# Feed-forward pairs of a two-block kernel: four special steps of eight, banks drained by ScalarE and added by transfers

## The reference, cut to what matters

```python
D_FF = 4 * D_MODEL
        u = _rmsnorm(h, norm_mlp_g[layer])
        a = jnp.einsum('bsd,df->bsf', u, w_up[layer])
        a = jnp.square(jax.nn.relu(a))
        h = h + jnp.einsum('bsf,fd->bsd', a, w_down[layer])
    return _rmsnorm(h, norm_final_g)
```

## Time and profile before

| | |
|---|---|
| median of 3 runs | 2109.48 us (2109.46 to 2109.78) |
| the profiled execution's own time | 2109.17 us |
| its span in the profile | 2107.1 us |
| TensorE (PE) busy | 2087.0 us, 99% |
| VectorE (DVE) busy | 1442.8 us, 68% |
| ScalarE (ACT) busy | 1082.2 us, 51% |
| GpSimd (POOL) busy | 40.1 us, 2% |
| moved by DMA | 402.60 MB, 191 GB/s |
| granted TensorE clock | 0.999 of full speed |

### The profile page before, as it was taken

How to read it: one execution, slowest core, us unless ns; L and a number is a source line. 1 busy time by engine, 2 the same in 40 slices (tenths; PEclk the granted TensorE clock), 3 DMA queues, 4 the chain that set the end, 5 groups by cost and what they waited for, 6 DMA issues and landing times.

```text
span 2107.1 us, 24963 instructions
## 1 busy us (share of the span) xinstructions
PE 2087.0 (99%) x10059; PEld 1753.2 (83%) x10059; DVE 1442.8 (68%) x1872; ACT 1082.2 (51%) x1409; POOL 40.1 (2%) x50
## 2 busy tenths in 40 slices
PE   8999999999999999999999999999999999999998
PEld 6888888888888888888888888888888888888886
DVE  5878788875555776556554455566896796797684
ACT  5545555555444675554455454354544554454453
POOL 0000000000000020000000000000000000000000
PEclk9999999999999999999999999999999999999999
DMA  7555555465465544365745542455555465556552
GB/s 268 185 181 198 200 182 217 180 240 196 175 221 199 189 155 165 131 229 200 294 180 182 193 165 100 160 200 184 198 204 194 164 236 181 180 199 220 182 219 98
DMA packets 56563, 402.60 MB, mean 191 GB/s; under 512 B 6240, under 2 KB 6496, under 8 KB 9216
## 3 DMA queue, kind: packets, MB, share of 16 engines
q1 hardware_dynamic: 53648, 380.67, 50.4%
q0 software_dynamic: 2656, 19.81, 2.4%
q10 hardware_dynamic: 144, 0.52, 0.1%
HBM read 392.59 MB, written 8.39 MB: 190 GB/s over the span
## 4 chain that ended last, share of the span: by engine, by line
PE 96%; ACT 1%; DVE 1%; issue 1%; DMA 0%; SPq 0%; POOLq 0%; POOL 0%; DVEq 0%; ACTq 0%
PE proj L619 15%; PE proj L621 15%; PE proj L620 15%; PE proj L1083 11%; PE proj L1087 6%; PE proj L724 4%; PE proj L726 4%; PE proj L725 4%; PE tbank L724 2%; PE tbank L726 2%; PE tbank L725 2%; PE tbank L578 2%; PE bank_a L724 1%; PE bank_a L726 1%; PE bank_a L725 1%; PE bank_b L726 1%
## 5 line engine op out<-in xcount | busy, mean ns | idle before, releaser
L1730 DVE TENSOR_TENSOR w_lo<-raw,w_hi 128x1024 fp32r<-128x1024 f32 x630 | 747.2, 1199 | 522.8 <-ACT w_hi L1190 515.6
L1190 ACT ACTIVATE w_hi<-raw 128x1024 fp32r<-128x1024 f32 x630 | 648.0, 1040 | 755.9 <-PE proj L621 478.1
L619 PE MATMUL proj<-w_hi,a_both 128*128 128x512 f32 x1280 | 511.8, 400 | 0.0
L621 PE MATMUL proj<-w_hi,a_both 128*128 128x512 f32 x1280 | 499.8, 390 | 0.0
L620 PE MATMUL proj<-w_lo,a_both 128*128 128x512 f32 x1280 | 498.4, 389 | 0.0
L621 PEld LDWEIGHTS proj<-w_hi,a_both 128*128 128x128 f32 x1280 | 240.3, 188 | 51.7
L620 PEld LDWEIGHTS proj<-w_lo,a_both 128*128 128x128 f32 x1280 | 240.7, 188 | 47.5
L619 PEld LDWEIGHTS proj<-w_hi,a_both 128*128 128x128 f32 x1280 | 240.6, 188 | 46.9
L1083 PE MATMUL proj<-a_both,w_hi 128*128 128x512 f32 x672 | 160.6, 391 | 0.3 <-DVE a_both L1776 0.3
L1083 PEld LDWEIGHTS proj<-a_both,w_hi 128*128 128x128 f32 x672 | 123.5, 188 | 24.5 <-DVE a_both L1776 0.5
L1190 ACT ACTIVATE w_hi_deep<-raw 128x1024 fp32r<-128x1024 f32 x84 | 83.6, 1021 | 95.2 <-PE proj L1087 59.4
(11 more groups left out here) (523 smaller groups left out, 3002.3 us busy)
## 6 DMA issues: line engine op xcount, KB each, us to landing
raw<-stream SPq DMA_DIRECT2D x359, 1024.0 KB, 4.8
nat<-x SPq DMA_DIRECT2D x4, 512.0 KB, 8.5
z_store<-z POOLq DMA_DIRECT2D x1, 2048.0 KB, 8.3
ga_store<-z POOLq DMA_DIRECT2D x1, 2048.0 KB, 12.3
gb_store<-z POOLq DMA_DIRECT2D x4, 512.0 KB, 7.3
yb<-z_store POOLq DMA_DIRECT2D x4, 512.0 KB, 9.4
ga<-ga_store POOLq DMA_DIRECT2D x1, 2048.0 KB, 8.1
gb<-gb_store POOLq DMA_DIRECT2D x1, 2048.0 KB, 14.3
```

Source lines behind the costliest of these rows:

```text
L619: nc.tensor.matmul(banks[t][:, :], ah, wh, start=first, stop=False)
L621: last = nc.tensor.matmul(banks[t][:, :], al, wh, start=False, stop=end)
L1190: A(hi_places[s][:, 0:width], src, ACT.Copy).then_inc(w_rounded, 1)
L1730: V.tensor_tensor(lo_places[s][:, 0:width], src, hi_places[s][:, 0:width].bitcast(f32), SUB).then_inc(w_rest, 1)
```

## The change

`SUM_AT` becomes (1, 2, 4, 5) instead of (1, 2, 3): each of the seven pairs has a fourth special step, and the last is step 5 instead of step 3. The sums of hidden values of the fourth lie in tiles of their own, and the sums of the steps 4 and 5 are made in chunks 5 and 6 of the up stage.

The reading of the banks is done otherwise. ScalarE copies each whole bank, scaled, to a tile of its own (`drain_whole`), and GpSimd starts a transfer that adds the tile to the residual (`accum_op=ADD`). Mixed bank 0 goes that way too. The other three sums of mixed banks stay with VectorE, in another order, two of them behind the last read of a mixed bank. The four tiles are the staging tiles that the up stage and `add_mixed` use too (`drain`), so ScalarE's drain of bank 3, into the tile of `u`, waits for the end of VectorE's adds (`mixed_added`), and that of bank 0 for the landing of the mixed bank's transfer (`mixed_in`). Whoever writes such a tile next waits for the landing of its transfer (`wait_drains`).

```diff
-SUM_AT = (1, 2, 3)
+SUM_AT = (1, 2, 4, 5)
...
+        drain = {2: stg2[:, 1, :], 3: stg[:, 0, :], 0: stg2[:, 0, :], 1: stg[:, 1, :]}
...
@@ gpsimd
-            pool.wait_ge(w_rest, FIRST_PIECE[SUM_UNITS[-1]] + 4)
-            pool.dma_start(fg[:, :], fg_in).then_inc(fg_in_s, 16)
+            for q in range(PAIRS):
+                if q == PAIRS - 1:
+                    pool.wait_ge(w_rest, FIRST_PIECE[SUM_UNITS[-1]] + 4)
+                    pool.dma_start(fg[:, :], fg_in).then_inc(fg_in_s, 16)
+                n1 = 2 * (q % 2)
+                out_of = lambda o: nat[:, o // 2, (n1 + o % 2) * CW:(n1 + o % 2 + 1) * CW]
+                pool.wait_ge(mixed_scaled, q + 1)
+                pool.dma_start(out_of(0), drain[0], accum_op=ADD).then_inc(mixed_in, 16)
+                pool.wait_ge(mixed_added, q + 1)
+                for i, o in enumerate(END_ORDER):
+                    pool.wait_ge(part_read, 5 * (PAIRS_IN + q) + 2 + i)
+                    if o == 0:
+                        pool.wait_ge(mixed_in, 16 * (q + 1))
+                    pool.dma_start(out_of(o), drain[o], accum_op=ADD).then_inc(whole_in[o], 16)
@@ scalar
+            def wait_drains(q):
+                for o in END_ORDER:
+                    act.wait_ge(whole_in[o], 16 * q)
+
+            def drain_whole(q):
+                act.wait_ge(part_read, 5 * (PAIRS_IN + q) + 1)
+                for i, o in enumerate(END_ORDER):
+                    if i < 3:
+                        act.wait_ge(part_done, 3 * (PAIRS_IN + q) + i + 1)
+                    else:
+                        act.wait_ge(w_used, done.at(RING + 2))
+                    if o == 3:
+                        act.wait_ge(mixed_added, q + 1)
+                    if o == 0:
+                        act.wait_ge(mixed_in, 16 * (q + 1))
+                    A(drain[o], parts[q % 2][o][:, :], ACT.Copy, scale=inv3_sq[:, o // 2:o // 2 + 1]).then_inc(part_read, 1)
...
                             if q % 2:
-                                act.wait_ge(part_read, 5 * (PAIRS_IN + q - 1) + 1)
+                                wait_drains(q)
...
-                            A(stg[:, 0, :], parts[1 - q % 2][0][:, :], ACT.Copy).then_inc(m_copied, 1)
+                            m = parts[1 - q % 2][0][:, :]
+                            A(drain[0], m, ACT.Copy, scale=inv3_sq[:, 0:1]).then_inc(mixed_scaled, 1)
+                            A(stg[:, 0, :], m, ACT.Copy).then_inc(m_copied, 1)
+                    if step == STEPS - 1:
+                        drain_whole(q)
                     pieces(4 if step in SUM_AT else 2, slot=slot)
...
                         if n and c == 0 and j == 3:
-                            act.wait_ge(part_read, 5 * (PAIRS_IN + 2 * n))
+                            wait_drains(2 * n)
@@ vector, add_mixed
-                    V.scalar_tensor_tensor(out(0, 0), u, inv3_sq[:, 0:1], out(0, 0), MUL, ADD).then_inc(dve_seq, 1)
...
+                    chain(V.tensor_tensor(u, mixed[2][:, :], u, ADD))
+                    V.tensor_tensor(w, mixed[1][:, :], u, ADD).then_inc(dve_seq, 1)
                     seq.add()
...
+                else:
+                    dve.wait_ge(dve_seq, seq.at())
+                    V.tensor_tensor(u, mixed[3][:, :], u, ADD).then_inc(dve_seq, 1)
                     seq.add()
...
+                    chain(V.scalar_tensor_tensor(out(0, 1), w, inv3_neg[:, 0:1], out(0, 1), MUL, ADD))
                     V.tensor_tensor(w, mixed[1][:, :], u, ADD).then_inc(part_read, 1)
+                    V.scalar_tensor_tensor(out(1, 0), u, inv3_neg[:, 1:2], out(1, 0), MUL, ADD)
                     dve.wait_ge(part_read, 5 * (PAIRS_IN + q) + 1)
+                    V.scalar_tensor_tensor(out(1, 1), w, inv3_sq[:, 1:2], out(1, 1), MUL, ADD).then_inc(mixed_added, 1)
...
-            def add_whole(q):
...
-                        if step == SUM_AT[-1] + 2 and j == 0:
-                            add_mixed(q, 2)
-                    if step == STEPS - 1:
-                        add_whole(q)
```

More of the change, by code:

```diff
@@ L243, in build @@
         w_lo_deep = place("w_lo_deep", [P, 2, PIECE], f32r, 152.25)
[L244 to L248, removed]
+        ms_at = [160.25 + 4 * i for i in range(3)] + [190.25]
+        ms_hi = [place(f"ms_hi{i}", [P, 4, P], f32r, ms_at[i]) for i in range(len(SUM_AT))]
+        ms_lo = [place(f"ms_lo{i}", [P, 4, P], f32r, ms_at[i] + 2) for i in range(len(SUM_AT))]
+        ms = place("ms", [P, 4, P], f32, 172.25)
+        w_sum = place("w_sum", [P, 2, 2 * PIECE], f32, 174.25)
+        fg = place("fg", [P, D], f32, 174.25)
         hi_places = [w_hi[:, i, :] for i in range(RING)] + [w_hi_deep[:, i, :] for i in range(2)]
@@ L445, in build @@
         whole_added = sem("whole_added")
+        mixed_scaled = sem("mixed_scaled")
+        mixed_in = sem("mixed_in")
+        mixed_added = sem("mixed_added")
+        whole_in = [sem(f"whole_in{o}") for o in range(4)]
         out_ready = sem("out_ready")
@@ L1132, in pair @@
                         i = SUM_AT.index(step)
-                        sum_step(2 * step, whole, mixed, m_hi, m_lo, ms_hi[:, i], ms_lo[:, i], sums.at(i + 1), i == 0,
+                        sum_step(2 * step, whole, mixed, m_hi, m_lo, ms_hi[i], ms_lo[i], sums.at(i + 1), i == 0,
                                  i == len(SUM_AT) - 1)
@@ L1639, in round_sums @@
                 act.wait_ge(ms_summed, ms_sums.at(i + 1))
-                A(ms_hi[:, i, :, :], ms[:, :, :], ACT.Copy).then_inc(ms_rounded, 1)
+                A(ms_hi[i][:, :, :], ms[:, :, :], ACT.Copy).then_inc(ms_rounded, 1)
+            def wait_drains(q):
[13 more added lines that the diff above has]
+                    A(drain[o], parts[q % 2][o][:, :], ACT.Copy, scale=inv3_sq[:, o // 2:o // 2 + 1]).then_inc(part_read, 1)
             def chunk_squares(c):
@@ L1690, in slot @@
                 if j in (3, 5):
-                    act.wait_ge(part_read, 5 * (PAIRS_IN + PAIRS))
+                    wait_drains(PAIRS)
                     chunk_squares((j - 3) // 2)
@@ L2405, in add_mixed @@
                     dve.wait_ge(w_used, done.at(RING))
-                    wait(dve, part_read, 5 * (PAIRS_IN + q))
                     dve.wait_ge(m_copied, PAIRS_IN + q + 1)
-                    V.scalar_tensor_tensor(out(0, 0), u, inv3_sq[:, 0:1], out(0, 0), MUL, ADD).then_inc(dve_seq, 1)
-                    seq.add()
[L2410 to L2414, removed]
+                    if q % 2:
+                        dve.wait_ge(whole_in[1], 16 * q)
@@ L2415, in add_mixed @@
+                    if q > 1:
+                        for o in END_ORDER:
+                            dve.wait_ge(whole_in[o], 16 * (q - 1))
+                    chain(V.tensor_tensor(u, mixed[2][:, :], u, ADD))
+                    V.tensor_tensor(w, mixed[1][:, :], u, ADD).then_inc(dve_seq, 1)
+                    seq.add()
+                else:
+                    dve.wait_ge(dve_seq, seq.at())
+                    V.tensor_tensor(u, mixed[3][:, :], u, ADD).then_inc(dve_seq, 1)
                     seq.add()
-                    chain(V.scalar_tensor_tensor(out(1, 0), u, inv3_neg[:, 1:2], out(1, 0), MUL, ADD))
@@ L2417, in add_mixed @@
-                if part == 2:
+                    chain(V.scalar_tensor_tensor(out(0, 1), w, inv3_neg[:, 0:1], out(0, 1), MUL, ADD))
                     V.tensor_tensor(w, mixed[1][:, :], u, ADD).then_inc(part_read, 1)
+                    V.scalar_tensor_tensor(out(1, 0), u, inv3_neg[:, 1:2], out(1, 0), MUL, ADD)
                     dve.wait_ge(part_read, 5 * (PAIRS_IN + q) + 1)
-                    V.scalar_tensor_tensor(out(1, 1), w, inv3_sq[:, 1:2], out(1, 1), MUL, ADD).then_inc(dve_seq, 1)
-                    seq.add()
```

3 lines of the change are left out of this document (2 added, 1 removed).

## The result

The changed kernel takes 2118.32 us (median of 6, 2115.75 to 2119.16), the kernel before 2109.45 beside it: ratio 1.004, 95% interval 1.003 to 1.005. It is slower by 0.4%; the forecast was 2115.4 and slower. The profiled execution took 2115.75 us with a span of 2114.0 us; the time is 6.6 us and the span 6.9 us more than before. The other executions lie up to 3.4 us above it, where those of before lie within 0.8 us of each other. The six times go with the mean granted clock: 2115.8 twice with 0.999, 2117.6 with 0.998, 2119.1 three times with 0.997.

What follows compares the result with a forecast made beforehand. TensorE, busy 99% of the span, was taken to bound the kernel, with VectorE nearly as full; 4.76 us saved against three holes of 2.22 and three of 1.34 gave +5.9, so 2115.4 us, range 2107 to 2122.

Steps and rivals of the forecast that it cites:

- The gain: One more special step in each of 7 pairs saves 3 matmuls of 0.2267 us each: 4.76 us in all.
- The even hole: End of pairs 0, 2, 4: TensorE waits for VectorE's last read of a mixed bank, 2.2 us, three times.
- T: Start of the first matmul of a pair's step 6; the next pair is due at T + 10.88 us.
- The odd hole: End of pairs 1, 3, 5: the up stage waits for ScalarE's second drain, behind VectorE's last two adds, 1.3 us, three times.
- The splits behind the drains: ScalarE's last splits in a pair are held behind the drains; priced at nothing, least margin found 1.3 us.
- the sums in the up stage: Operand sums cost VectorE 2 us more a slab, priced at nothing; only 0.6 us comes through to the pair.
- The transfers: The mixed bank's adding transfer must land before the third drain; it may take 12.5 us, priced at nothing.
- Rival (c): Transfers come late, perhaps because VectorE locks GpSimd out: 2121.5 us at 14.5 us each, some 30 us more at 22.4; chance 0.13.
- The sum: -4.76 + 3 x 2.22 + 3 x 1.34 = +5.9 us on the profiled execution's 2109.17.
- TensorE's holes of 2 us I give no clock price: Holes at the pairs' ends cost only their length; granted clock read 1.00 in the first 20 us, TensorE busy 11.3.
- (a): Rival: the reads are over before the pair is, only the saving in matmuls is left, 2104.7 us; chance 0.12.
- (b): Rival: one kind of hole only, or half of each; only even 2111.4 us, only odd 2108.8; chance 0.2.

Runs made afterwards that it cites:

- experiment 4: The change with all reading of the mixed banks at once behind step 6's first split in every pair, second set of weight sums behind it: 2104.49 us.
- Experiment 2: The change, with the next pair's second set of weight sums behind the reading of the mixed banks in even pairs: 2108.35 us.
- experiment 6: The change, with the first addition of the second set of weight sums made three times, ahead of the reading: 2128.93 us.
- experiment 7: The change with the reading at once behind step 6's first split in all pairs, both sets of weight sums still ahead of it: 2110.3 us.
- Experiment 3: The change, with both parts of the reading at once behind step 6's first split in odd pairs only: 2114.82 us.
- experiment 1: The change with special steps at (1, 2, 3) again, keeping ScalarE's drains and the adding transfers: 2108.98 us.
- experiment 8: The change again, unchanged, for more executions: 2117.05 us (2115.2 to 2118.81).
- 5: The kernel before with special steps at (1, 2, 4, 5), all reading in step 6, no drains or transfers: 2130.99 us.
- 9: The kernel before with special steps at (1, 2, 4, 5), reading at once, second weight sums behind it, no drains or transfers: 2122.39 us.

## Why the prediction was right, and where it was not

*The gain.* Right: 21 matmuls fewer, and the kernel of experiment 4 gives 4.8 us, the 4.76 of the sum.

*The even hole, 2.2 us three times.* Right: 2.27 by starts. The chain of VectorE's rows was 14.9 us in the forecast and took 14.9 (1526.33 to 1541.18). But VectorE had not caught up, as the forecast had it by 0.2 us: the chain began at T - 1.8 instead of T - 2.1, so the last read ended at T + 13.1 for T + 12.8. TensorE then followed at once instead of 0.26 later. That the two errors nearly cancel is luck. Experiment 2 takes one link of 2.6 us out and the hole goes; experiment 6 puts 2.5 in and it grows by 2.5; experiment 7 takes a half split of 0.6 out and the wait falls from 2.1 to 1.6.

*The odd hole, 1.3 us three times.* Right: 1.22 by starts, by the path named, VectorE's last two adds, then ScalarE's second drain. Experiment 3 takes it away by the adds alone. The drain itself was mis-sized: 0.67 to 0.69 us with a scale from a tile, where the plain copy's 0.58 was taken.

*What was priced at nothing.* The splits behind the drains and the sums in the up stage: right, no wait for split weights came up in the pairs. The transfers: right in effect. The page gives, issue to landing:

```profile
nat<-stg POOLq DMA_DIRECT2D x35, 256.0 KB, 5.6
```

The mixed bank's took 5.8 to 7.6 us, well inside the 12.5 that were allowed. The Trainium skill, page "DMA: Bandwidth & Descriptors", section "Anatomy of one DMA — SWDGE (gpsimd) path", fits 2.0 us and bytes over 436 GB/s to a transfer, by which an estimate for this one is 2.6 us; the trace has more than twice that, for an adding transfer between places of the on-chip memory, and decides. Rival (c), with the starved descriptors, did not come: with VectorE full in the even pairs, ScalarE waited for a landing once in the run, 0.4 us.

*The sum.* 5.9 us were forecast for an execution in which the clock stands, 6.6 measured. The holes are 0.3 of the 0.7: 3.65 us a block for 3.56, where the starts show 3.49 in the holes and the rest is the wider spacing of the first matmuls behind them. The up stages are 0.4, 3 x 0.13, where the forecast had nothing. They go with the fourth special step and not with the drains: experiment 1 has 89.04 us, as before, experiment 4 has 89.17. What in the stage takes them was not looked into. The 0.24 ahead of the first pair and 0.3 less between span and time cancel.

*The step that failed* is "TensorE's holes of 2 us I give no clock price". It rested on the granted clock of 1.00 that the windows print for the first 20 us, and that figure could not bear it. TensorE's timeline of the kernel before has matmuls of one shape there, with no wait between them:

```profile
16.91 0.41 PE L679 MATMUL proj<-a_both,w_hi 128*128 128x256 f32 x1
17.12 0.41 PE L680 MATMUL proj<-a_both,w_lo 128*128 128x256 f32 x1
17.34 0.36 PE L678 MATMUL proj<-a_both,w_hi 128*128 128x256 f32 x1
17.53 0.28 PE L679 MATMUL proj<-a_both,w_hi 128*128 128x256 f32 x1
17.65 0.28 PE L680 MATMUL proj<-a_both,w_lo 128*128 128x256 f32 x1
```

Up to 17.34 they start 0.21 us apart, from 17.53 on 0.12, nearly the ratio of 0.43 to 0.23 in experiment 8. By the spacing, TensorE came out of its half idle start at the lower level, whatever the windows print.

In 8 of the 11 executions of the change seen here the mean clock and the time show one or more falls, for some 1.6 us each; that is most of why the median lies 2.9 us above the forecast, in the upper part of its range. That the falls belong to the holes is shown: none in the 22 executions of experiments 1 and 4, without holes, nor in the 11 of experiment 2, with waits of 1.1 us; none that lengthened one of 11 at 1.6; one or more in 8 of 11 of the change at 2.1, and in all 10 of experiment 3, with the same even waits. Hole by hole in the profiled executions: none of 12 at 1.1 us (the change, experiments 2, 6 and 8), none of 3 at 1.6, 2 of 9 at 2.1 (one each in 3 and 8, none in the change), 5 of 6 at 2.5 to 2.6 (5 and 9), and all 6 at 3.7 and 4.6 (5 and 6). Transfers don't do it alone: experiments 1 and 4 have them and no falls, 5 and 9 have falls and no adding transfers. What decides it for a single hole of 2.1 us stays open, and so does why experiment 3 had more falls than the change. The Trainium skill, page "TensorE: Matmul & The Clock Gate", section "HAM oscillation — how this bites in real kernels", has it that TensorE is throttled behind idle gaps and that the matmuls that follow pay for it. The trace agrees, with 0.43 for 0.23 us. The waits in that section's example are of 3 to 5 us; here 2.1 us were at times enough.

*The rivals.* (a), the reads over before the pair is, became true in experiment 4 (2104.5 for its 2104.7): it needed another order, not shorter instructions. (b) is experiment 2 with the odd holes alone (2108.35 for 2108.8) and experiment 3 with the even ones alone (2114.8 for 2111.4, of it some 3 us falls of the clock). The change has both kinds. The forecast gave 0.6 to slower.

## What to carry to other kernels

Where a change takes work from the bounding engine, look for the next handover behind it and write out, row by row, what the neighbour's queue holds ahead of the instruction that hands over; its total load says little. Here 2.6 us of additions that nobody needed yet stood ahead of reads that TensorE waited for. Putting them behind took the change from 0.4% slower to no difference (experiment 2); with the reading at once in every pair as well it is 0.2% faster (experiment 4), all with the same work. Give a hole in a dense row of matmuls a price above its length once it nears 2 us. Check the clock that a window prints against the spacing of matmuls of one shape.

## What the runs showed that was not expected

The granted clock falls behind holes of about 2.1 us in some executions and not in others of the same kernel, so that the kernel has a ladder of times some 1.6 us apart (2115.2 to 2115.8, 2116.6 to 2117.6, 2118.8 to 2119.2); with waits of 1.1 us it never did in the 11 executions of experiment 2, and with 4.6 us it did behind all three in the profiled execution. A spread of times beside a quiet kernel before was the first sign of it.

An adding transfer takes GpSimd longer to issue than a plain load, 0.83 us and more against 0.57, and 256 KB of it land in a median of 5.6 us; whether that is for the adding or for the places that it moves between is not shown. Thirty-five of them beside a stream that by itself takes 0.55 to 0.58 of the DMA engines in the pairs cost the kernel nothing that can be told (experiment 1).
